# Split weights of a two-layer decoder trunk: the lo parts start 128 bytes further on, modulo 512, than the hi parts

## What is computed

```
proj = einsum('bsd,de->bse', h, w_in)             # 2048 x 6144
y    = silu(layernorm(conv(a * sigmoid(b)))) * silu(z)
x    = x + einsum('bse,ed->bsd', y, w_out)        # 2048 x 2048
kv   = einsum('bsd,de->bse', rmsnorm(x), w_kv)    # 2048 x 12288
qz   = einsum('bsd,de->bse', rmsnorm(x), b_w_in)  # 2048 x 8192
x    = x + einsum('bse,ed->bsd', merged_attention * silu(z), b_w_out)
out  = rmsnorm(x)
```

## Time and profile before

| what | value |
|---|---|
| median of 3 runs | 1480.65 us (1480.16 to 1481.35) |
| the profiled execution | 1480.8 us |
| its span, first to last instruction | 1479.0 us |
| mean granted TensorE clock | 0.998 |
| busy: PE, PEld | 98%, 95% |
| busy: DVE, ACT, POOL | 54%, 47%, 26% |

### The profile page before, as it was taken

One profiled execution on the slowest core, in us unless ns is written; L12 is line 12 of the kernel. 1 busy time (PEld: TensorE's weight loads), 2 busy tenths in 40 slices (PEclk: granted clock), 3 DMA queues, 4 the chain that ended last, 5 costly groups with the idle time before them and its releaser, 6 DMA issues.

```text
span 1479.0 us, 28343 instructions
## 1 busy us (share of the span) xinstructions
PE 1451.4 (98%) x11475; PEld 1409.2 (95%) x11475; DVE 793.1 (54%) x1232; ACT 690.1 (47%) x989; POOL 385.4 (26%) x168
## 2 busy tenths in 40 slices
PE   6999999999999999999999999999999999999997
PEld 5999999988899999999999999999999999999886
DVE  3899998422545455454554545545454454544333
ACT  5444444675644444444444444444444444443543
POOL 5788888788300000000000000000000000000595
PEclk9999999999999999999999999999999999999999
DMA  9666666556596665666656666566665666653752
GB/s 267 174 193 176 181 191 183 173 188 208 165 291 183 171 181 162 188 181 171 181 163 188 182 170 181 160 188 183 171 181 160 189 182 171 181 159 107 256 199 86
DMA packets 455090, 268.52 MB, mean 182 GB/s; under 512 B 4491, under 2 KB 437211, under 8 KB 454668
## 3 DMA queue, kind: packets, MB, share of 16 engines
q1 hardware_dynamic: 454860, 267.96, 62.8%
q10 hardware_dynamic: 192, 0.05, 0.0%
HBM read 263.70 MB, written 4.29 MB: 181 GB/s over the span
## 4 chain that ended last, share of the span: by engine, by line
issue 76%; POOL 18%; PE 5%; POOLq 0%; DVE 0%; ACT 0%
POOL w_lo L303 18%; PE bank L344 2%; PE bank L346 2%; PE bank L345 2%; POOLq L302 0%; ACT bank L745 0%; DVE y L1069 0%; DVE resid L1053 0%; PE bank L1244 0%; ACT y L766 0%; PE bank L377 0%; PE bank L375 0%; PE bank L376 0%; PE bank L1246 0%; ACT stat L761 0%
## 5 line engine op out<-in xcount | busy, mean ns | idle before, releaser
L294 ACT ACTIVATE w_hi<-raw 128x1024 fp32r<-128x1024 f32 x478 | 505.4, 1061 | 517.3 <-PE bank L326 453.6
L303 POOL TENSOR_TENSOR w_lo<-raw,w_hi 128x1024 fp32r<-128x1024 f32 x160 | 384.5, 2414 | 1077.0 <-ACT w_hi L294 1062.7
L324 PE MATMUL bank<-mem_a,w_hi 128*128 128x256 f32 x2304 | 649.0, 282 | 4.6 <-POOL w_lo L303 1.7
L325 PE MATMUL bank<-mem_a,w_hi 128*128 128x256 f32 x2304 | 643.9, 279 | 0.0
L326 PE MATMUL bank<-mem_a,w_lo 128*128 128x256 f32 x2304 | 640.8, 278 | 0.0
L303 DVE TENSOR_TENSOR w_lo<-raw,w_hi 128x1024 fp32r<-128x1024 f32 x320 | 390.3, 1225 | 417.3 <-ACT w_hi L294 417.3
L324 PEld LDWEIGHTS bank<-mem_a,w_hi 128*128 128x128 f32 x2304 | 432.4, 188 | 8.1 <-POOL w_lo L303 3.0
L325 PEld LDWEIGHTS bank<-mem_a,w_hi 128*128 128x128 f32 x2304 | 435.9, 189 | 0.1
L326 PEld LDWEIGHTS bank<-mem_a,w_lo 128*128 128x128 f32 x2304 | 432.4, 188 | 0.0
L324 PE MATMUL bank<-mem_b,w_hi 128*128 128x256 f32 x1024 | 287.7, 281 | 0.0
L325 PE MATMUL bank<-mem_b,w_hi 128*128 128x256 f32 x1024 | 286.0, 279 | 0.0
(11 more groups left out here) (151 smaller groups left out, 961.0 us busy)
## 6 DMA issues: line engine op xcount, KB each, us to landing
raw<-w_kv_dram SPq DMA_DIRECT2D x96, 1024.0 KB, 6.0
raw<-b_w_in_dram SPq DMA_DIRECT2D x64, 1024.0 KB, 6.6
raw<-a_w_in_dram SPq DMA_DIRECT2D x47, 1024.0 KB, 5.9
raw<-a_w_out_dram SPq DMA_DIRECT2D x16, 1024.0 KB, 5.1
raw<-b_w_out_dram SPq DMA_DIRECT2D x16, 1024.0 KB, 5.0
bias<-bias_dram SPq DMA_DIRECT2D x16, 384.0 KB, 7.9
x_sb<-x_dram SPq DMA_DIRECT2D x4, 512.0 KB, 5.7
resid_dram<-x_sb SPq DMA_DIRECT2D x1, 2048.0 KB, 11.4
```

The source lines that it names most:

```text
L294: nc.scalar.activation(w_hi[:, stream.half_slot(half), :], raw[:, slot, part:part + HALF], ACT.Copy).then_inc(hi_done, 1)
L303: eng.tensor_tensor(w_lo[:, stream.half_slot(half), :], raw[:, slot, part:part + HALF], w_hi[:, stream.half_slot(half), :].bitcast(F32), A ...
L324: nc.tensor.matmul(dst[:, 0:S], wide_hi, source(kt, 0), start=(kt == 0), stop=False)
L325: nc.tensor.matmul(dst[:, 0:S], wide_hi, source(kt, 1), start=False, stop=False)
```

## The change

128 bytes (32 floats) are put between `w_hi` and `w_lo`, and the unused `gap` ahead of `stat` grows by 384 bytes (96 floats). `w_lo`, `ident`, `mean_w`, `vectors` and `taps` so move on by 128 bytes, and `stat` and all that follows it by 512 bytes. After it `w_hi` and all the inputs lie where they did modulo 512, and each lo tile begins at 128 modulo 512. The four small tensors between `w_lo` and `gap` move with `w_lo`, though the description says that everything else keeps its place. No instruction is added, removed or moved, and no wait.

```
@@ -136,12 +136,13 @@
         raw = sb("raw", [P, RAW_SLOTS, SLAB])
         sq_scrap, r_row, rk_row = shared(("sq_scrap", [P, CHUNK], F32), ("r_row", [P, S], F32), ("rk_row", [P, S], F32))
         w_hi = sb("w_hi", [P, HALF_SLOTS, HALF], F32R)
+        sb("lo_gap", [P, 32])
         w_lo = sb("w_lo", [P, HALF_SLOTS, HALF], F32R)
         ident = sb("ident", [P, P])
         mean_w = sb("mean_w", [P, P])
         vectors = sb("vectors", [P, VECTORS, KT])
         taps = sb("taps", [P, TAPS, KT])
-        sb("gap", [P, 16])
+        sb("gap", [P, 112])
         stat = sb("stat", [P, 32])
```

## The result

| | before | after |
|---|---|---|
| median | 1480.41 us (4 runs) | 1497.53 us (4 runs, 1496.79 to 1498.03) |
| the profiled execution | 1480.8 us, span 1479.0 | 1498.0 us, span 1496.2 |

The ratio is 1.0113, with a 95% interval of 1.0101 to 1.0125. The forecast was no change, 1480.6 us, in a range to 1485.0. It was wrong: the kernel is 17 us slower, beyond every case that was priced on that side.

What follows compares the result with a forecast made beforehand. The prediction took TensorE's own pace to bound the kernel. Every term, for TensorE's lo reads, the writers and the moved small tensors, was 0, giving 1480.6 us (chance 0.70, own range 1478.5 to 1483; 8 in 10: 1475.5 to 1485.0).

Steps and rivals of the forecast that it cites:

- every case that was priced on that side: Slower rivals: double price 8.3 us (chance 0.09), POOL's subtraction 5.8 us (0.03), moved small tensors (0.02).
- What bounds the kernel: Whole kernel: TensorE's own pace, PE busy all 660.00 us of the heads, VectorE full in stage AB.
- a price that hangs on the distance of a load and a stream alone is thus the same sum before and after: Lo tiles as weights (L326, 3328 times): 16 tiles meet the same eight distances twice each, so 0 us.
- The estimate of 0.003 us per triple: Column projections: most that the shift could change each of 3328 triples, 10.0 us faster or slower in all.
- a price of tile 4: Slab of the column projections: tile 4 took 0.36 us, read as a tile effect of at most 0.01 that averages out.
- The lo tiles as stream: Output projections (L345 and L376, 256 times): at most 0.8 us faster or slower, taken as 0.
- The writers and the small tensors: VectorE's and POOL's lo subtractions, and ident and taps at their new places: cost taken as 0.
- Rival "hi and lo loads collide": Column projections: successive loads at 0 modulo 512 collide, the shift parts them; 10.0 us faster, 1470.6, chance 0.16.
- Rival "met twice": Column projections: a bad distance stalls hi and lo loads on separate tiles; 8.3 us slower, 1488.9, chance 0.09.

Runs made afterwards that it cites:

- the products alone: Kernels with none of the reference's work, only TensorE products on constant tiles, in segments with different places: 0.1133 to 0.1200 us per product by places of weights and stream.
- the second kernel of products: Only TensorE products on constant tiles, with further places of hi, lo and inputs than the first such kernel; lo at 128 took 0.16 us more per 96 products than at 0.

## Why the prediction was wrong, point by point

- **What bounds the kernel.** Right: TensorE's pace, at a granted clock of 1.00, and in AB VectorE close beside it. The prediction didn't draw the consequence that a slower PE first fills its 2.4 us of waits in AB; the stage lost 0.2 us.
- **The step that failed** is "a price that hangs on the distance of a load and a stream alone is thus the same sum before and after". The sum over the tiles does cancel, and the products alone show a price that goes with that distance (5.67 to 5.97 us for 48). But the price isn't a sum over pairs: 5.86 is what the pairs give for the triples, 5.82 and 5.90 are what they take. Which place follows which counts, and how the run begins, and the evenly spread distances gave no protection. The estimate of 0.003 us per triple was too small as well; the measured one is 0.08/16 = 0.005.
- **A row that was read wrongly** is the step of 0.36 in the earlier trace rows beside the 0.35 in the earlier trace rows. The prediction took it for a price of tile 4. But that slab is the first one behind the transposes of v, of which the view shows the last four:

```profile
1012.73 0.60 PE L1225 MATMUL bank<-ident,v_t 128*128 128x128 f32 x4
```

  In the next slab, that of the earlier trace rows, no tile stands out. It was a sign that the products hadn't settled yet behind an interruption, and it couldn't bound what the places can cost. With the measured 0.005 us per triple, 3328 x 0.005 = 17 us on either side was open.
- **The lo tiles as stream** were bounded at 256 x 0.003. But all 768 products of 512 columns became slower, by (1.40 - 1.36)/6 = 0.007 us on the mean, some 5 us if nothing hid them; from the first to the last start 2.2 us can be read in the projection of layer 0 and (1481.5 - 1394.9) - (1464.3 - 1379.0) = 1.3 in that of layer 1. In the changed projection the three kinds have steps of 0.24, 0.23 and 0.23, 0.2333 on the mean, where each had 0.2267: more than the moved read pays, and only that one was priced.
- **The writers and the small tensors** at 0: right. The kernel in which both are moved and TensorE's reads are not has 1480.5 us.
- **Rival "hi and lo loads collide" (faster):** went the other way. With lo at 0 hi and lo loads begin at the same place and that is the faster layout. The prediction named this as the one pair that doesn't cancel, and priced it in one direction only. In the products alone the alternating weights fall on both sides of their pairs.
- **Rival "met twice":** the right side, with its sign (5.62 or more, the writers as before), and 8.3 us where 17 came. Its mechanism, one stall that hides another, isn't shown by these runs; that the order of places has a part is.
- **The two pages of the Trainium skill.** SBUF — State Buffer, section "Who interferes with whom", has PE never wait on anyone, and TensorE: Matmul & The Clock Gate, section "Step-by-step: what each phase is for", two independent read ports. No other engine was needed for the loss, so the first isn't contradicted as far as other engines go; but a product with its load takes 0.1133 to 0.1200 us by the places of weights and stream, so two ports didn't make their places indifferent. The prediction applied the gap of columns/2.4 + 2.5 ns to products in a row. The Trainium skill, in the same page's section "Back-to-back issue gap", gives it for an isolated product, and has the spacing of a stream of loads and products set by both; the 116.7 ns of the earlier trace rows are such a stream.

What stays open is the rule inside TensorE: whether distances or places count, what part the load has, why a run keeps its pace, and what a restart must be like to end in the fast one. The segments map it for these places and interruptions, and even these don't carry over to the kernel one for one.

## What to carry to other kernels

Where TensorE bounds a kernel and each product has its own weights, the places of weights and stream are part of its time, some 6% between the best and the worst of the places in steps of 32 bytes here. A layout can't be priced by adding up pairs. A run of products alone, in the kernel's own order and after interruptions like the kernel's, shows the paces that a layout can take, and one short kernel does it for fifty layouts. Which of them the kernel takes has to be read from the kernel's own slabs. Prefer a layout whose pace doesn't change with what came before, unless the fast pace has been seen to hold after every interruption that the kernel has.

## What the runs showed of the hardware that was not expected

- The pace goes with the places of weights and stream: with inputs in the layout of before, 64 or 128 bytes more for the lo weights alone cost the kernel 13 or 17 us; 256 bytes cost nothing (1481.0 us in one run, and 1481.0 before).
- A few paces return in many segments: 0.1133, 0.1167, 0.1178, 0.1183, 0.1189 and 0.1200 us per product of 256 columns. Others stand between and beyond them: 0.1173 for a stream at 160, and 0.1217 with all inputs at 196 (231.79 in the second kernel of products, 6.06 us for 48), 4 bytes from the place with 0.1133.
- One and the same row of products settles at one of two paces (0.1133 and 0.1178 with all inputs at 192) and keeps it until it is interrupted.
